# A two-layer decoder trunk on one core: where a schedule puts the third branch's norm steps, the compression steps and the tiles of stages 8 to 11

## The chip, the cores and the metric

The kernel runs on one core of one Trainium2 chip. The metric is device time in microseconds (us) for one execution of the whole program, taken from the first to the last work of that core. The engines are named PE (TensorE, matrix products), PEld (its weight loads), DVE (VectorE), ACT (ScalarE), POOL (GpSimd) and SP (SyncE, which only issues DMA transfers here).

## The reference, cut to what matters

Two layers. In each, h is the RMS-normed input (512 tokens x 1024), and one wide projection of h feeds three token mixers: A (8 heads with a forget gate), B (compressed, selected and windowed attention, 8 query heads on 2 key groups) and C (4 heads, each the difference of two softmax maps). Each mixer's output is multiplied by a SiLU gate, projected to 1024 columns, weighted by a sigmoid gate and summed; then an output projection, a residual and a gated per-layer embedding.

```
k_cmp = compress_blocks(kcb..., w1_k, w2_k)      # silu(flat @ w1 + b1) @ w2, likewise for v
w = prob[:, :, 0] - lam * prob[:, :, 1]          # branch C, lam = exp(..) - exp(..) + lam_init
yc = rmsnorm(out, subln_g) * (1.0 - lam_init)    # the third branch's norm, per head
merged = g0 * (ya @ w_br_a) + g1 * (yb @ w_br_b) + g2 * (yc @ w_br_c)
```

All products are to have fp32 accuracy. The kernel splits each operand into a high and a low part of a faster type and multiplies three times: high by high, low by high, high by low.

## The kernel before

**Tiles.** The dense work is cut into tiles of 128 output columns over all 512 tokens. A tile of a projection of h has 8 steps, a tile of a branch projection (`bra`, `brb`, `brc`) 4; a step is three matmuls of 512 columns (lines 729 to 731). A tile of the compression's hidden layer (`w1k`, `w1v`) has 4 steps of two matmuls of 256 columns (lines 742 and 743). Weights come from DRAM into `raw` (4 slots); ACT copies them to `w_hi` (line 1031, function `hi`), DVE subtracts to get `w_lo` (line 1260, function `lo`), each in two halves, into 2 slots. The weights of tile t+2 are therefore split only when tile t has ended. The output banks `D0` and `D1` alternate too: tile t+2 can't begin before tile t has been taken out of its bank (`arena`, `zs`, `rx` and `th` are such destinations; a `brb` tile is taken out by two DVE instructions, lines 1435 and 1439, which multiply by the gate and add to `acc`).

**Stages.** Twelve stages, 0 to 3 for branch A, 4 to 7 for B, 8 to 11 for C. In a stage the attention rows of one head pair run (`S` scores, softmax row maximum on DVE line 1511 and exponential on ACT line 1146, `T` transposes of the probabilities and their copy `pT`, line 541, `V` the product with the values, `N` the scaling into `y_q`), and between them the steps of the dense tiles that `dense_tiles` lists for the stage. Branch C also has `CB` (four DVE instructions, lines 1522 to 1525, that combine the two maps), `SQ` (ACT squares), `MS` (DVE takes the mean square, line 1575, and POOL raises it to the power -1/2, line 687), `YN` (four small DVE instructions and one multiplication of `y_q`, lines 1579 to 1583), `Y` (PE transposes `y_q`, line 934, DVE writes `y_f`) and `YS` (ACT and DVE split `y_f` into `y_hi` and `y_lo`, lines 1165 and 1597). Tiles whose columns are rotated (`qb`, `ksb`, `kwb`, `qc`, `kc`) have `swap` (4 DMAs and a POOL product) and `rot` later on.

**What sets the order.** `make_schedule` writes one list of items for all engines, and each engine issues its part of the list strictly in that order. A stage is cut into ticks, one per row (stage 11 has 7 more). Each tick places its row items and, spread between them, a share of the stage's dense steps by weight: a `w1k` or `w1v` step weighs 1, any other 2. Items in `late`, `newton` and `vq` are due at a tick; items in `follow` are due after a number of dense steps. So how much PE work lies between two items, and what stands before a given item in the queues of DVE and ACT, both come from this function.

Of the kernel before, what the change touches and what calls it, by code (L numbers as in the profile page):

```python
# [1723 lines left out]
```

## Time and profile before

| | us |
|---|---|
| median of 3 runs | 1573.89 (1573.87 to 1575.48) |
| the profiled execution, its own time | 1574.78 |
| its span, first to last instruction | 1573.0 |
| PE busy | 1514.2 (96%) |
| DVE busy | 941.8 (60%) |
| ACT busy | 638.6 (41%) |
| POOL busy | 73.4 (5%) |

PE is busy nearly all the time, so its idle time and the stretches at a lower granted clock are all that an order of work can change. A row of a timeline gives the start, the duration, the engine, the line and the operands, and in brackets how long the engine had been idle and what ended that. Matmul rows last longer than the distance between them, since matmuls overlap. Layer 1 runs from about 15 to 790 us, layer 2 after it, with the same order of items.

### The profile page before, as it was taken

Reading aid. Unit: us, or ns where it says so; the run is one execution under the profiler, and the core shown is the slowest. Engines: PE = TensorE matmul, PEld = TensorE weight load, DVE = VectorE, ACT = ScalarE, POOL = GpSimd, SP = SyncE. Lnnn points to the kernel's source line nnn. Section 1 sums busy time; section 2 is a strip of 40 time slices with the busy share of each in tenths; the row PEclk is TensorE's granted clock in tenths of the full one; section 3 lists DMA queues with packets and bytes.
Section 4 is the critical chain, followed back from the end, with each engine's and each line's share of the span. In section 5 each row is a group of like instructions: output and inputs, shape, how many; then the busy total and the mean of one; then the engine's idle time right before and its main releaser. Section 6 shows DMA issues by size and latency. Waiting matters only on the chain.

```text
span 1573.0 us, 22642 instructions
## 1 busy us (share of the span) xinstructions
PE 1514.2 (96%) x7957; PEld 1212.5 (77%) x7957; DVE 941.8 (60%) x2205; ACT 638.6 (41%) x1492; POOL 73.4 (5%) x79
## 2 busy tenths in 40 slices
PE   8999999999999999999999999999999999999997
PEld 6777777777777777878787777787887777788785
DVE  6856655555557666455576657655555666754544
ACT  6533433333344443343444334333434434433343
POOL 1000000000000000000200000000000000000011
PEclk9999999999999999999999999999999999999998
DMA  7223322222223332332442324222222233233222
GB/s 194 81 81 88 94 71 58 60 68 61 66 63 94 88 81 74 93 114 59 113 108 68 101 67 109 71 52 66 61 61 74 68 94 84 71 89 105 87 78 77
DMA packets 250300, 129.47 MB, mean 82 GB/s; under 512 B 45691, under 2 KB 245973, under 8 KB 250197
## 3 DMA queue, kind: packets, MB, share of 16 engines
q1 hardware_dynamic: 250196, 128.13, 30.5%
q8 instruction: 60, 0.98, 0.3%
q14 instruction: 44, 0.35, 0.1%
HBM read 118.67 MB, written 2.10 MB: 77 GB/s over the span
## 4 chain that ended last, share of the span: by engine, by line
PE 78%; DVE 8%; issue 6%; ACT 4%; DMA 1%; POOL 1%; SPq 1%; ACTq 0%; POOLq 0%; DVEq 0%
PE D L729 22%; PE D L731 19%; PE D L730 19%; PE Ob L917 7%; PE S L876 4%; PE T L895 3%; DVE w_lo L1260 2%; ACT w_hi L1031 1%; ACT probs L1146 1%; PE Ob L922 1%; DMA rs<-rx 1%; PE Mb L934 1%; SPq L630 1%; DVE h_lo L1602 1%; PE Mb L843 1%
## 5 line engine op out<-in xcount | busy, mean ns | idle before, releaser
L729 PE MATMUL D<-h_hi,w_hi 128*128 128x512 f32 x1264 | 544.6, 431 | 17.3 <-DVE zs L1408 4.9
L731 PE MATMUL D<-h_lo,w_hi 128*128 128x512 f32 x1264 | 496.8, 393 | 0.0
L730 PE MATMUL D<-h_hi,w_lo 128*128 128x512 f32 x1264 | 495.6, 392 | 0.0
L1260 DVE TENSOR_TENSOR w_lo<-raw,w_hi 128x512 fp32r<-128x512 f32 (+2 forms) x504 | 297.3, 631 | 315.5 <-ACT w_hi L1031 315.3
L1031 ACT ACTIVATE w_hi<-raw 128x512 fp32r<-128x512 f32 (+2 forms) x504 | 266.3, 575 | 315.4 <-PE D L731 314.4
L729 PEld LDWEIGHTS D<-h_hi,w_hi 128*128 128x128 f32 x1264 | 238.8, 189 | 82.0 <-issue 20.6
L1146 ACT ACTIVATE probs<-probs,nmax 128x128 f32<-128x128 f32 (+3 forms) x256 | 141.9, 555 | 376.3 <-DVE nmax L1511 376.2
L731 PEld LDWEIGHTS D<-h_lo,w_hi 128*128 128x128 f32 x1264 | 238.0, 188 | 53.4
L730 PEld LDWEIGHTS D<-h_hi,w_lo 128*128 128x128 f32 x1264 | 239.7, 190 | 30.8 <-issue 0.5
L1511 DVE CUSTOM_DVE_ANT_0 probs<-S,maskb 128x128 f32<-128x128 f32 (+3 forms) x256 | 115.2, 487 | 57.3 <-PE S L876 35.8
L541 DVE COPY pT<-T 128x128 f32<-128x128 f32 (+3 forms) x160 | 77.5, 486 | 50.0 <-PE T L895 49.6
L917 PEld LDWEIGHTS Ob<-v_b,pT 128*128 128x128 f32 x640 | 90.8, 191 | 11.9 <-ACT pT L539 0.9
L895 PE MATMUL T<-ident,probs 128*128 128x128 f32 x560 | 97.7, 272 | 1.7 <-ACT probs L1146 1.7
L876 PE MATMUL S<-arena 64*128 64x384 f32 (+3 forms) x768 | 93.8, 349 | 0.9 <-DVE arena L1404 0.9
L729 PE MATMUL D<-y_hi,w_hi 128*128 128x512 f32 x224 | 94.0, 420 | 0.4 <-DVE y_lo L1597 0.4
L895 PEld LDWEIGHTS T<-ident,probs 128*128 128x128 f32 x560 | 72.6, 140 | 27.1 <-ACT probs L1146 4.0
L876 PEld LDWEIGHTS S<-arena 64*128 64x128 f32 x768 | 57.1, 185 | 45.6 <-issue 41.2
L731 PE MATMUL D<-y_lo,w_hi 128*128 128x512 f32 x224 | 87.9, 392 | 0.0
L730 PE MATMUL D<-y_hi,w_lo 128*128 128x512 f32 x224 | 87.5, 390 | 0.0
L917 PE MATMUL Ob<-v_b,pT 128*128 128x64 f32 x640 | 85.4, 264 | 0.0
L684 POOL TENSOR_TENSOR rb<-rs,sinT 128x512 f32<-128x512 f32 x28 | 36.1, 1290 | 1012.9 <-DMA rs<-rx 595.2
L917 PEld LDWEIGHTS Ob<-v_ac,pT 128*128 128x128 f32 x480 | 66.9, 192 | 16.3 <-DVE pT L541 9.1
(241 smaller groups left out, 1497.8 us busy)
## 6 DMA issues: line engine op xcount, KB each, us to landing
raw<-in_w_in_dram SPq DMA_DIRECT2D x124, 512.0 KB, 3.9
raw<-in_w_in_dram SPq DMA_DIRECT2D x32, 256.0 KB, 3.7
raw<-in_w_out_dram SPq DMA_DIRECT2D x16, 512.0 KB, 4.0
raw<-in_w_ple_gate_dram SPq DMA_DIRECT2D x16, 512.0 KB, 4.2
rs<-rx SPq DMA_DIRECT2D x80, 64.0 KB, 2.0
raw<-in_cmp_w_k_dram SPq DMA_DIRECT2D x8, 512.0 KB, 3.7
raw<-in_cmp_w_v_dram SPq DMA_DIRECT2D x8, 512.0 KB, 3.8
raw<-in_w_br_a_dram SPq DMA_DIRECT2D x16, 256.0 KB, 2.8
```

What stands on the lines that cost most here:

```text
L541: eng.tensor_copy(pT[:, k % 2, 0:n], Tr[k % 2][:, 0:n]).then_inc(M["pt_dve_s"], 1)
L684: pool.tensor_tensor(rb[:], rs[:], sinT[:], ALU.mult).then_inc(M["pool_rot"], 1)
L729: pe.matmul(o, w_hi[:, sl, cs], hi[:, k, :], start=(k == 0), stop=False)
L730: pe.matmul(o, w_lo[:, sl, cs], hi[:, k, :], start=False, stop=False)
L731: ins = pe.matmul(o, w_hi[:, sl, cs], lo[:, k, :], start=False, stop=last)
L876: ins = pe.matmul(Sc[h][:, 0:n], qx[ps, qs], kx[ps, 0:n], start=(step == 0), stop=last)
L895: ins = pe.transpose(Tr[k % 2][:, j * P:(j + 1) * P], src[:, j * P:(j + 1) * P], ident[:])
L917: ins = pe.matmul(Ob[:, oc], pT[:, k % 2, j * P:(j + 1) * P], vs(j), start=(j == 0), stop=(j == i))
L1031: A(w_hi[:, sl, half], raw[:, ring(L, t, RAW), half], ACT.Copy).then_inc(M["act_hi"], 1)
L1146: A(probs[:, r % NP_, 0:n], probs[:, r % NP_, 0:n], ACT.Exp, scale=-1.0, bias=nmax[:, r % 8:r % 8 + 1], accum_out=sums[:, u % 2, i, c:c + ...
L1260: TT(w_lo[:, sl, half], raw[:, ring(L, t, RAW), half], f(w_hi[:, sl, half]), ALU.subtract).then_inc(M["dve_lo"], 1)
L1511: dve.tensor_tensor_reduce(probs[:, r % NP_, 0:n], Sc[r % 2][:, 0:n], maskb[:, S - n:S], -1.0, 3.0e38, ALU.add, ALU.min, nmax[:, r % 8:r % ...
```

## The change

The code is the same in what it computes. Five things differ.

1. Stages 7 to 11 hold other tiles. `kc 1` moves from stage 8 to stage 7. Stages 8, 9 and 10 go from 48 dense steps to 36 each, and stage 11 from 32 to 60. The last tile is now `brb 7`, and `zc 3` stands in the middle of stage 11, so that `Y` and `YS` of unit 11 come inside the list and the extra wait on line 945 goes.
2. `MS` and `YN` of branch C are placed 3 and 5 dense steps after the last `N` of a unit (before: both one tick later), `Y` still two ticks later; for unit 11 too.
3. The last lambda arithmetic on DVE becomes an item `lam` of its own, 30 steps after the `fg` tile instead of 7. ACT's exponential for it stays at `gates`.
4. A `w1k` or `w1v` step weighs 4, not 1, in the share of a tick. `ht` and `kcmp` come 12 and 16 steps after `w1k 3`, not 4 and 7.
5. A `brb` tile waits for the addition of the one before it.

```
-    st[7] = [("qc", 0), ("zb", 3), ("kc", 0), ("mga", 6), ("bra", 6), ("mga", 7), ("bra", 7)]
-    st[8] = [("qc", 1), ("mgb", 0), ("kc", 1), ("zc", 0), ("brb", 0), ("mgb", 1), ("brb", 1)]
-    st[9] = [("qc", 2), ("mgb", 2), ("kc", 2), ("zc", 1), ("brb", 2), ("mgb", 3), ("brb", 3)]
...
-    st[11] = [("mgb", 6), ("brb", 6), ("mgb", 7), ("brb", 7), ("zc", 3)]
+    st[7] = [("qc", 0), ("zb", 3), ("kc", 0), ("mga", 6), ("bra", 6), ("kc", 1), ("mga", 7), ("bra", 7)]
+    st[8] = [("qc", 1), ("mgb", 0), ("zc", 0), ("brb", 0), ("mgb", 1)]
+    st[9] = [("qc", 2), ("brb", 1), ("kc", 2), ("zc", 1), ("mgb", 2)]
...
+    st[11] = [("brb", 3), ("mgb", 4), ("brb", 4), ("zc", 3), ("mgb", 5), ("brb", 5), ("mgb", 6), ("brb", 6),
+              ("mgb", 7), ("brb", 7)]
...
-                follow.extend([[3, ("lf1", t)], [7, ("gates", t)], [9, ("lf2", t)]])
+                follow.extend([[3, ("lf1", t)], [7, ("gates", t)], [9, ("lf2", t)], [30, ("lam", t)]])
...
-                follow.extend([[4, ("ht", t)], [7, ("kcmp", t)]])
+                follow.extend([[12, ("ht", t)], [16, ("kcmp", t)]])
...
-            weight.append(weight[-1] + (1 if tiles[t][0] in ("w1k", "w1v") else 2))
+            weight.append(weight[-1] + (4 if tiles[t][0] in ("w1k", "w1v") else 2))
...
-                            late.append((tick + 1, ("MS", u)))
-                            newton.append((tick + 1, ("YN", u)))
-                            if u < UNITS - 1:
-                                late.append((tick + 2, ("Y", u)))
+                            late.append((tick + 2, ("Y", u)))
...
                     follow.append([1, ("SQ", part[1])])
+                    if i == NQ - 1:
+                        follow.extend([[3, ("MS", u)], [5, ("YN", u)]])
...
-    items += [("Y", UNITS - 1), ("YS", UNITS - 1)]
...
-                                if j == 0:
-                                    pe.wait_ge(M["dve_evac"], dve_evac.after(T0 - 2))
...
+                                if not first and n:
+                                    dve.wait_ge(M["dve_acc"], n)
```

DVE's queue in stage 9, around the norm of unit 8. `msq` is the norm's small arithmetic, `y_q` the unit's output, `coef` and `probs` the combination of the next unit's two maps, `rc` and `arena` a rotated tile. Before:

```order
L1523 TENSOR_TENSOR coef<-coef,lams 128x1
L1524 TENSOR_SCALAR probs<-probs,coef 128x256
L1525 SCALAR_TENSOR_TENSOR probs<-probs,coef 128x256
L1500 TENSOR_TENSOR rc<-rc,rb 128x512
L1502 TENSOR_TENSOR arena<-rc,arena 128x512
L541 COPY pT<-T0 128x128
L1575 TENSOR_SCALAR msq<-msq 128x4
L1579 TENSOR_TENSOR msq<-msq 128x4
L1580 TENSOR_TENSOR msq<-msq 128x4
L1581 TENSOR_SCALAR msq<-msq 128x4
L1582 TENSOR_TENSOR msq<-msq 128x4
L1583 TENSOR_TENSOR y_q<-y_q,msq 128x512
```

The same place after the change, from the end of tile `brb 1` (its `w_lo`, `qf` and `acc`):

```order
L1258 TENSOR_TENSOR w_lo<-raw,w_hi 128x512 x2
L1435 SCALAR_TENSOR_TENSOR qf<-th,D0 128x512
L1439 TENSOR_TENSOR acc<-acc,qf 128x512
L1523 RECIPROCAL coef<-sums 128x2
L1524 TENSOR_TENSOR coef<-coef,lams 128x1
L1525 TENSOR_SCALAR probs<-probs,coef 128x256
L1526 SCALAR_TENSOR_TENSOR probs<-probs,coef 128x256
L1576 TENSOR_SCALAR msq<-msq 128x4
L541 COPY pT<-T0 128x128
L1580 TENSOR_TENSOR msq<-msq 128x4
L1581 TENSOR_TENSOR msq<-msq 128x4
L1582 TENSOR_SCALAR msq<-msq 128x4
```

The rotated tile's two instructions have gone behind the norm, and the four that end a `brb` tile now stand before it.

DVE's queue at the norm of unit 11, near the end of stage 11. Before:

```order
L1575 TENSOR_SCALAR msq<-msq 128x4
L1260 TENSOR_TENSOR w_lo<-raw,w_hi 128x512 x2
L1435 SCALAR_TENSOR_TENSOR qf<-th,D1 128x512
L1439 TENSOR_TENSOR acc<-acc,qf 128x512
L1579 TENSOR_TENSOR msq<-msq 128x4
L1580 TENSOR_TENSOR msq<-msq 128x4
L1581 TENSOR_SCALAR msq<-msq 128x4
L1582 TENSOR_TENSOR msq<-msq 128x4
L1583 TENSOR_TENSOR y_q<-y_q,msq 128x512
L1597 TENSOR_TENSOR y_lo<-y_f,y_hi 128x512 x3
```

After:

```order
L1258 TENSOR_TENSOR w_lo<-raw,w_hi 128x512 x2
L1576 TENSOR_SCALAR msq<-msq 128x4
L1580 TENSOR_TENSOR msq<-msq 128x4
L1581 TENSOR_TENSOR msq<-msq 128x4
L1582 TENSOR_SCALAR msq<-msq 128x4
L1583 TENSOR_TENSOR msq<-msq 128x4
L1584 TENSOR_TENSOR y_q<-y_q,msq 128x512
L1258 TENSOR_TENSOR w_lo<-raw,w_hi 128x256 x2
L1435 SCALAR_TENSOR_TENSOR qf<-th,D0 128x512
L1439 TENSOR_TENSOR acc<-acc,qf 128x512
L1593 SCALAR_TENSOR_TENSOR y_f<-Mb,gsc,zs 128x512
```

Nothing is left between the mean square and the four small instructions, and `Y` follows inside the list; before it came behind all dense steps of the stage.

PE's queue around the first hidden tile `w1k 0`, in layer 1. Before, the row `Ob` is `V` and the two rows `S` are the next unit's scores:

```order
L917 MATMUL Ob<-v_ac,pT 128x64 x3
L742 MATMUL D<-w_hi,arena 128x256
L743 MATMUL D<-w_lo,arena 128x256
L742 MATMUL D<-w_hi,arena 128x256
L743 MATMUL D<-w_lo,arena 128x256
L742 MATMUL D<-w_hi,arena 128x256
L743 MATMUL D<-w_lo,arena 128x256
L742 MATMUL D<-w_hi,arena 128x256
L743 MATMUL D<-w_lo,arena 128x256
L876 MATMUL S<-arena 128x128 x6
L882 MATMUL S<-ck,selr 128x128 x2
L729 MATMUL D<-h_hi,w_hi 128x512
```

After, from the end of tile `za 0` on:

```order
L731 MATMUL D<-h_lo,w_hi 128x512
L876 MATMUL S<-arena 128x512 x6
L882 MATMUL S<-ck,selr 128x512 x2
L895 MATMUL T<-ident,probs 128x128 x3
L742 MATMUL D<-w_hi,arena 128x256
L743 MATMUL D<-w_lo,arena 128x256
L917 MATMUL Ob<-v_ac,pT 128x64 x3
L742 MATMUL D<-w_hi,arena 128x256
L743 MATMUL D<-w_lo,arena 128x256
L895 MATMUL T<-ident,probs 128x128 x4
L917 MATMUL Ob<-v_ac,pT 128x64 x3
L742 MATMUL D<-w_hi,arena 128x256
```

The scores of the unit's last row, two transposes and a `V` have come in behind `za 0`; the four-matrix transpose needs the probabilities of the scores four items ahead of it.

## Rows read from the trace of the kernel before

**Rows 1.** The page: busy time by engine, and one group (busy, mean ns | idle before).

```profile
PE 1514.2 (96%) x7957; PEld 1212.5 (77%) x7957; DVE 941.8 (60%) x2205; ACT 638.6 (41%) x1492; POOL 73.4 (5%) x79
...
L729 PE MATMUL D<-y_hi,w_hi 128*128 128x512 f32 x224 | 94.0, 420 | 0.4 <-DVE y_lo L1597 0.4
```

**Rows 2.** Waits of PE, whole span: us in total, times, longest us.

```profile
PE Mb L934 <- DVE y_q L1583: 7.4, 6, 1.3
...
PE D L729 <- DVE zs L1408: 4.9, 4, 2.5
PE Ob L917 <- DVE pT L541: 4.8, 5, 1.8
PE Mb L816 <- DVE tmp L1430: 4.6, 2, 2.3
PE D L729 <- DVE arena L1404: 3.7, 5, 1.3
```

**Rows 3.** Timeline of PE, stage 11 and the step behind it, layer 1.

```profile
603.77 0.38 PE L917 MATMUL Ob<-v_ac,pT 128*128 128x128 f32 x1 [1.81 <-DVE pT L541]
...
617.79 0.49 PE L729 MATMUL D<-h_hi,w_hi 128*128 128x512 f32 x1 [1.00 <-ACT th L1093]
```

**Rows 4.** Timeline of all engines where a `brb` tile ends, stage 9.

```profile
497.24 0.39 PE L730 MATMUL D<-y_hi,w_lo 128*128 128x512 f32 x1
...
497.47 0.39 PE L731 MATMUL D<-y_lo,w_hi 128*128 128x512 f32 x1
...
497.95 1.15 ACT L1031 ACTIVATE w_hi<-raw 128x512 fp32r<-128x512 f32 x2 [1.43 <-PE D L731]
...
498.62 1.29 DVE L1260 TENSOR_TENSOR w_lo<-raw,w_hi 128x512 fp32r<-128x512 f32 x2 [1.25 <-ACT w_hi L1031]
...
499.83 0.68 DVE L1435 SCALAR_TENSOR_TENSOR qf<-th,D 128x512 f32<-128x512 f32 x1
...
500.54 0.69 DVE L1439 TENSOR_TENSOR acc<-acc,qf 128x512 f32<-128x512 f32 x1
```

**Rows 5.** Timeline of all engines at the norm of unit 8, stage 9.

```profile
514.52 0.16 DVE L1522 RECIPROCAL coef<-sums 128x2 f32<-128x2 f32 x1
...
515.29 0.49 DVE L1525 SCALAR_TENSOR_TENSOR probs<-probs,coef 128x256 f32<-128x256 f32 x1
...
517.85 0.79 PE L876 MATMUL S<-arena 64*128 64x384 f32 x6
...
517.94 0.16 DVE L1575 TENSOR_SCALAR msq<-msq 128x4 f32<-128x4 f32 x1
...
519.23 0.16 DVE L1579 TENSOR_TENSOR msq<-msq 128x4 f32<-128x4 f32 x1 [1.13 <-POOL msq L687]
...
520.86 0.63 PE L934 MATMUL Mb<-ident,y_q 128*128 128x128 f32 x4 [1.33 <-DVE y_q L1583]
```

**Rows 6.** Timelines of DVE and ACT at the end of `za 0`.

```profile
84.26 0.69 DVE L1511 CUSTOM_DVE_ANT_0 probs<-S,maskb 128x512 f32<-128x512 f32 x1 [0.38 <-PE S L882]
...
85.00 0.72 ACT L1146 ACTIVATE probs<-probs,nmax 128x512 f32<-128x512 f32 x1 [2.91 <-DVE nmax L1511]
...
89.45 1.15 ACT L1031 ACTIVATE w_hi<-raw 128x512 fp32r<-128x512 f32 x2 [2.93 <-PE D L731]
...
91.32 0.68 DVE L1408 SCALAR_TENSOR_TENSOR zs<-th,D 128x512 f32<-128x512 f32 x1
```

**Rows 7.** Timelines of DVE, PE and ACT: the compression's input, and `w1k 3`.

```profile
73.40 3.00 DVE L1355 TENSOR_TENSOR v_b<-D,par 64x248 f32<-64x248 f32 x8
...
139.66 0.47 PE L729 MATMUL D<-h_hi,w_hi 128*128 128x512 f32 x1 [0.27 <-DVE arena L1404]
...
139.89 0.51 ACT L1146 ACTIVATE probs<-probs,nmax 128x256 f32<-128x256 f32 x1 [1.29 <-DVE nmax L1511]
```

**Rows 8.** Stretches: length, busy PE, PEld, DVE, ACT, POOL, then granted clock, DMA, GB/s.

```profile
197.00:204.00 7.00, 5.99 (x21) 5.01 (x22) 3.82 (x9) 0.89 (x2) 0.00 (x0) 0.76 0.66 150
918.00:924.00 6.00, 5.67 (x24) 4.52 (x25) 2.26 (x8) 0.00 (x0) 0.00 (x0) 0.72 0.28 81
```

**Rows 9.** Timeline of all engines, stage 8.

```profile
482.49 1.29 POOL L684 TENSOR_TENSOR rb<-rs,sinT 128x512 f32<-128x512 f32 x1 [11.20 <-DMA rs<-rx]
...
483.08 1.25 DVE L1597 TENSOR_TENSOR y_lo<-y_f,y_hi 128x512 fp32r<-128x512 f32 x1 [1.65 <-ACT y_hi L1165]
```

More of the change, by code:

```diff
@@ L76, in dense_tiles @@
     st[6] = [("qb", 3), ("vc", 2), ("zb", 2), ("vc", 3), ("mga", 4), ("bra", 4), ("mga", 5), ("bra", 5)]
-    st[7] = [("qc", 0), ("zb", 3), ("kc", 0), ("mga", 6), ("bra", 6), ("mga", 7), ("bra", 7)]
-    st[8] = [("qc", 1), ("mgb", 0), ("kc", 1), ("zc", 0), ("brb", 0), ("mgb", 1), ("brb", 1)]
-    st[9] = [("qc", 2), ("mgb", 2), ("kc", 2), ("zc", 1), ("brb", 2), ("mgb", 3), ("brb", 3)]
-    st[10] = [("qc", 3), ("mgb", 4), ("kc", 3), ("zc", 2), ("brb", 4), ("mgb", 5), ("brb", 5)]
-    st[11] = [("mgb", 6), ("brb", 6), ("mgb", 7), ("brb", 7), ("zc", 3)]
+    st[7] = [("qc", 0), ("zb", 3), ("kc", 0), ("mga", 6), ("bra", 6), ("kc", 1), ("mga", 7), ("bra", 7)]
+    st[8] = [("qc", 1), ("mgb", 0), ("zc", 0), ("brb", 0), ("mgb", 1)]
+    st[9] = [("qc", 2), ("brb", 1), ("kc", 2), ("zc", 1), ("mgb", 2)]
+    st[10] = [("qc", 3), ("brb", 2), ("kc", 3), ("zc", 2), ("mgb", 3)]
+    st[11] = [("brb", 3), ("mgb", 4), ("brb", 4), ("zc", 3), ("mgb", 5), ("brb", 5), ("mgb", 6), ("brb", 6),
+              ("mgb", 7), ("brb", 7)]
     return st
@@ L174, in emit_group @@
             if kind == "fg":
-                follow.extend([[3, ("lf1", t)], [7, ("gates", t)], [9, ("lf2", t)]])
+                follow.extend([[3, ("lf1", t)], [7, ("gates", t)], [9, ("lf2", t)], [30, ("lam", t)]])
             if kind == "brb" and tiles[t][1] == 7:
-                for u in range(8, 11):
+                for u in range(8, UNITS):
                     follow.append([1 + u - 8, ("YS", u)])
@@ L188, in make_schedule @@
         emit_group(g)
-    vq, late, newton = [], [], []
+    vq, late = [], []
     tick = 0
@@ L226, in make_schedule @@
                         if branch(u) == "C":
-                            late.append((tick + 1, ("MS", u)))
-                            newton.append((tick + 1, ("YN", u)))
-                            if u < UNITS - 1:
-                                late.append((tick + 2, ("Y", u)))
+                            late.append((tick + 2, ("Y", u)))
                         else:
                             late.append((tick + 1, ("Y", u)))
-            while newton and newton[0][0] <= tick:
-                parts.append(newton.pop(0)[1])
             if s == 8 and 1 <= j <= 4:
@@ L242, in make_schedule @@
                 if part[0] == "N" and branch(part[1] // NQ) == "C":
+                    u, i = divmod(part[1], NQ)
                     follow.append([1, ("SQ", part[1])])
+                    if i == NQ - 1:
+                        follow.extend([[3, ("MS", u)], [5, ("YN", u)]])
                     follow.sort(key=lambda f: f[0])
@@ L259, in make_schedule @@
         items.append(follow.pop(0)[1])
-    items += [("Y", UNITS - 1), ("YS", UNITS - 1)]
-    assert not late and not newton and not vq and ti == len(prob_rows)
+    assert not late and not vq and ti == len(prob_rows)
     where = {x: n for n, x in enumerate(items)}
     for u in range(8, UNITS):
-        assert where[("SQ", NQ * u + NQ - 1)] < where[("MS", u)], u
+        assert where[("SQ", NQ * u + NQ - 1)] < where[("MS", u)] < where[("YN", u)] < where[("Y", u)], u
+        assert where[("Y", u)] < where[("YS", u)], u
+    assert tiles[-2][0] == "mgb" and tiles[-1][0] == "brb"
     for u in range(1, UNITS):
@@ L1461, in _ @@
                             link(TT(gsc[:], par[:, PAR_SUB + L:PAR_SUB + L + 1], lconst[:, 1:2], ALU.mult))
+                        elif what == "lam":
                             dve.wait_ge(M["act_lam"], L + 1)
```

## The prediction, made before the changed kernel was run

> **What bounds the kernel now.** I read the page first, then the list of waits of PE, then the timelines round each wait. The page shows PE busy 96% of the span, the other engines 60% or less [rows 1]; no work of PE is added or taken away by the change, so only its waits and its clock can move. The list of waits shows what they are [rows 2]: six before the transpose of `y_q` (7.4 us), four for `zs`, five for `pT`, two for the hidden layer's `tmp` (4.6), five for `arena`. In stage 11 and right behind it stand one of 1.81 for a copy of probabilities and one of 1.00 for a gate tile [rows 3], and both layers have them. The stretches view shows two dips of the granted clock, to means of 0.76 and 0.72 [rows 8]. That is TensorE at its lower level (1.2 GHz) for part of the stretch, behind a wait of 2.5 for `zs` in layer 1 and of 2.3 for `tmp` in layer 2 [rows 2]. Each costs (1 - 0.76) x 7 = (1 - 0.72) x 6 = 1.7 us.
>
> The question for every moved item is whether the engine that feeds PE there is free. Where a tile ends, ACT and DVE are not, and that is the core of my sum. A matmul of 512 columns starts 0.23 after the one before (497.24, 497.47), so a step of three takes 0.70, and PE is free of the `brb` tile at 497.70; ACT's split starts at 497.95, DVE's two `w_lo` at 498.62, `qf` at 499.83, and `acc` ends at 501.23 [rows 4]. So **DVE is free of a `brb` tile 3.5 us after PE is**.
>
> **The norm of units 8 and 9 (stages 9 and 10).** From the end of `brb 1`, DVE has: the tile's end 3.5; `coef` to `probs` 1.26 (514.52 to 515.78); the mean square 0.16; its wait for POOL, which lasts from 518.10 to 519.23 and hides the 0.28 copy of `pT`, 1.13; from there to PE's transpose 1.63 (519.23 to 520.86) [rows 5]. Sum 7.7. PE has from the same point to `Y`: seven steps, 4.9, one `S` pass of 0.8 and a small transpose of 0.1 [rows 4, 5]: 5.9. The wait becomes 1.8; before it is 1.33 [rows 5]. Before, the rotation's two instructions stood in front of the mean square; now a `brb` tile's end does, and PE has a shorter tick to cover it. Lower bound 0, if DVE starts the tile's end without delay and the copies overlap more than the rows show; upper 2.6, with POOL's product on top (below).
>
> The same shorter ticks leave DVE busy through the rest of the stage. Stages 9 and 10 lose 12 of 48 steps, 8.4 us of PE time each, but only an `mgb` and a `brb` tile's ends on DVE (1.3 and 2.2). Followed on, DVE copies the probabilities of the third row 0.9 us after PE wants them, behind `zs`, a rotation and a `coef` group. The rows give no such wait in these stages before, so its bounds are 0 and 2; I take 0.9. Together (1.8 + 0.9 - 1.33) = +1.37 per stage, x4: **+5.5**.
>
> **Stage 8.** `brb 0` waits for `y_lo` of unit 7: 0.2 per layer before [rows 1]. `YS 7` comes one step later and there are fewer steps between; the queue in front of it (a `y_lo`, two maxima, the rotation with its turn through ACT, `N`, the square, `y_hi`) sums to 7.9 after the end of `mgb 0`, PE arrives at 6.9. Wait 1.0, bounds 0.2 and 1.8: **+1.6** for both layers.
>
> **Stage 11.** Removed per layer: the 1.81, a 0.4 of the same kind, the 1.0 before `Y 10` and the 1.00 at the first `mgc` [rows 2, 3]; 4.3 in all. With four steps per tick instead of two the copies come in time. `zc 3` no longer ends the stage, and the new last wait, for `y_lo` of unit 11 before the first `brc`, is hidden: the tile's end and four `y_lo` take 5.3, the 8 steps of `mgc` 5.6. That cover is thin; if DVE is 0.5 late it costs 0.2. Added: `Y 10` has four steps fewer work before it than DVE needs (lo 2.2, `coef` 1.26, norm 2.9 against 4.4 of PE): 1.9. `Y 11` stands right behind `brb 6`: DVE has the two `w_lo` of `mgb 7`, free 2.2 after PE [rows 4], then 0.16 + 1.13 + 1.63 [rows 5], 5.1 in all, and PE only four steps, 2.8. Wait 2.3; before, it lay behind the whole of `zc 3` and cost nothing. Sum 4.2 against 4.3: **-0.3** for both layers, bounds -6 and +1.
>
> **Compression.** *Before `qa 2`, beside `w1k 0`*: a wait of 0.6 for `zs` goes (one of the four [rows 2]). But the transpose of the unit's last row now stands between two hidden steps. Its probabilities need `zs` (ends 92.00, 2.8 after PE left `za 0`), then a maximum of 0.69, then an exponential of 0.72 [rows 6]: 4.3. PE has `S` 1.3, transposes 0.3, `V` 0.65, two hidden steps 0.6: 2.8. Wait 1.4, so +0.8 per layer, +1.7. *`w1k 1`*: 0.4 of work comes in front of a wait for `arena`: -0.8 for both. *`w1k 3`*: `ht` 12 steps on removes 2.3 per layer [rows 2]. In its place the transposes of the row just scored stand in the hidden tile; they need an exponential that ends at 140.40, while before the next tile started at 139.66 [rows 7]; PE ends 1.1 later than before. Net -2.4. *`w1v`*: 0.43 of `V` in front of each wait for `zs`, and 0.2 near `ht`: -1.3. *`kcb`*: scores now stand right behind the tile whose eight DVE instructions take 3.00 [rows 7]; two waits of 0.6 replace one of 0.6 (layer 1) or two of 0.55 (layer 2): +0.7. Sum **-2.1**, bounds -9 (every wait named here gone) and +3.
>
> **Clock.** Without the 2.3 wait the dip of layer 2 should go; the wait for `zs` in layer 1 shrinks from 2.5 only to 2.0, and I leave that dip: **-1.7**, bounds -3.4 and +3.4 (the 2.3 before `Y 11` causes one per layer).
>
> **Lambda, and the wait on the addition.** 0. DVE's next instruction behind the lambdas waited for ACT's split in any case, which stands behind ACT's exponential, and that has not moved. The addition is always done.
>
> **A rule against it.** POOL's `rb` product ran from 482.49 to 483.78, and `y_lo`, which other rows show at 0.69, took 1.25 beside it and ended 0.55 after it [rows 9]. The Trainium skill, GPSIMD Engine Reference, section "Specifications", says that POOL's interfaces to SBUF are shared with VectorE and that they contend where a DVE instruction has two SBUF inputs. By that, with `rb` of `qc 2` now falling on the `acc` addition (two SBUF inputs), the norm waits of stages 9 and 10 would be up to 0.6 longer, +2.4 in all; without it, nothing. The sum stands without.
>
> **The sum**, against the profiled execution's own 1574.78: +5.5 +1.6 -0.3 -2.1 -1.7 = +3.0, so 1577.8; the median of the runs shown lies 0.9 lower, so 1576.9.
>
> **Rivals.** *A, DVE is not the late engine.* If the ends of `brb` tiles slip in front as fast as the steps, the norm waits go (-7.4), stage 11's copies and gate waits too (-6.4), with compression and clock as above (-3.8): 1556. For it: that DVE is busy only 60%, and DVE stands idle for over 1 us in front of most splits. Against it: those idle times lie before a tile's end, and the items in question all stand behind one. A half of it, where the norm waits halve (-3.7) and stages 8 to 10 get no other new ones, stage 11, compression and clock as in the sum (-4.1), gives 1566. *B, a pile-up, slower.* The place is the tick in stages 9 and 10 in which `zs`, a rotation and `coef` meet. It decides once DVE's queue of a stage with its waits is longer than PE's 33 us; I count 29. Each us of excess then stays, four times, with `rb` on top and a clock dip behind `Y 11` in each layer: 1573.9 +3.0 +2.4 +3.4 = 1582.7, more where the excess is larger. *C, no effect*: the waits only change place, each as long as it was: 1574.
>
> **How the numbers follow.** What a measurement can tell from no change is 0.2%, 3.1 us. My forecast, a sum of 0 to +6, gets 0.45, half of it within 0.2% and half beyond. Rival A with its half gets 0.28, B 0.15, C 0.12. Slower: 0.225 + 0.15, and a little of C, 0.39; same: 0.225 + 0.10, 0.33; faster 0.28. The range runs from 1563, between A and its half, to 1583, where B ends; the forecast's own is 1573 to 1580.
>
> **What would show it.** In the profile after: waits of PE for `y_q` of 1.8 in stages 9 and 10, 1.9 and 2.3 in stage 11, 8 of them; waits for `pT` of about 0.9 once in each of stages 9 and 10 and none of 1.8 in stage 11; the wait of the first `mgc` gone; one of 1.4 for `probs` beside `w1k 0` and about as much beside `w1k 3`; none for `tmp` of 2.3; one dip of the clock. I am wrong if waits for `y_q` sum to less than 7.4, or if those in stage 11 fall by over 2 per layer.

## The result, and the profile after

| | us |
|---|---|
| before, median of 7 runs beside the changed kernel | 1575.48 (1573.87 to 1578.6) |
| changed kernel, median of 7 runs | 1585.53 (1582.76 to 1592.05) |
| ratio, 95% interval | 1.0072 (1.0059 to 1.0086) |
| profiled executions, before and after | 1574.78 and 1591.31 |
| their mean granted clock | 0.995 and 0.986 |

The change costs 0.7%, outside the range I gave. The seven runs of the changed kernel lie further apart than those of before, and their time goes with the clock: 1591.3 and 1592.1 us at a mean of 0.986, 1588.4 at 0.988, 1585.0 to 1585.5 at 0.991, 1582.8 at 0.992. The profiled execution, 1591.31 us, is the second longest of the seven, 5.8 us above the median, so its profile shows more of the lower clock than a run at the median has.

The page shows the same work, 11.5 us more of it busy on PE. It answers to [rows 1]:

```profile
PE 1525.7 (96%) x7957; PEld 1220.2 (77%) x7957; DVE 946.6 (60%) x2205; ACT 638.4 (40%) x1492; POOL 74.4 (5%) x79
```

The instructions are equal in number, so the added busy time is not work; the granted clocks further down say what it is. The waits of PE, which answer to [rows 2] (us in total, times, longest us):

```profile
PE Mb L934 <- DVE y_q L1584: 18.2, 8, 2.6
PE T L895 <- ACT probs L1144: 6.9, 6, 1.4
...
PE D L729 <- DVE arena L1402: 2.3, 3, 1.3
PE Ob L917 <- DVE pT L541: 2.1, 4, 0.6
...
PE D L729 <- DVE y_lo L1598: 1.9, 2, 0.9
PE D L729 <- DVE zs L1406: 1.8, 2, 0.9
...
PE Ob L917 <- DVE y_q L1559: 1.2, 2, 0.6
```

The `tmp` line (4.6) and the wait of the first `mgc` [rows 3] are gone, `zs`, `pT` and `arena` have shrunk; `y_q` has gone from 7.4 to 18.2 and `probs` from 1.7 to 6.9. All idle times of PE over 0.06 us, summed, are 48.8 us before and 53.9 after: +5.1.

The other 11.4 of the 16.5 us are in the stretches view. Columns as in [rows 8], the last but two being the granted clock; the first two rows are the same times as those of [rows 8], now at full clock, as is everything from 99 to 515 us and from 877 to 1293; the others stand behind waits:

```profile
197.00:204.00 7.00, 6.12 (x36) 4.81 (x34) 4.50 (x10) 1.83 (x4) 0.00 (x0) 1.00 0.66 150
918.00:924.00 6.00, 4.61 (x35) 3.90 (x35) 3.72 (x11) 2.63 (x7) 0.00 (x0) 1.00 0.05 10
...
88.00:100.00 12.00, 10.58 (x55) 8.93 (x55) 7.05 (x19) 3.67 (x11) 0.00 (x0) 0.72 0.32 87
514.00:520.00 6.00, 5.52 (x21) 4.59 (x22) 5.19 (x13) 3.35 (x8) 0.00 (x0) 0.72 0.13 32
551.00:557.00 6.00, 5.25 (x19) 4.36 (x20) 5.18 (x11) 3.35 (x8) 0.00 (x0) 0.72 0.11 28
868.00:880.00 12.00, 10.58 (x52) 9.00 (x51) 6.35 (x18) 3.55 (x10) 0.00 (x0) 0.72 0.29 88
...
1364.00:1370.00 6.00, 5.19 (x19) 4.43 (x20) 5.82 (x15) 1.71 (x6) 0.00 (x0) 0.72 0.34 87
1394.00:1400.00 6.00, 4.70 (x16) 3.89 (x17) 3.67 (x9) 0.00 (x0) 0.00 (x0) 0.72 0.44 125
```

A mean of 0.72 over 6 us is 3.4 us at 1.2 GHz, worth 1.7 us of work at 2.4 GHz; the two rows of 12 us hold twice that. With 1292 to 1298 and 1329 to 1335, which read alike, there are ten such units, against two before. Eight more at up to 1.7 are up to 13.7; the busy time shows 11.5. Four of the ten stand behind norm waits of 2.60 to 2.65, four (two in a row, twice) behind the waits of 1.42 beside `w1k 0`, and one each, in layer 2 alone, behind the 1.63 before `Y 10` and the 2.19 before `Y 11`.

What they stand behind, with the norm of unit 8 first (all engines, stage 9; it answers to [rows 5]), then the transpose beside `w1k 0`:

```profile
510.51 0.16 DVE L1576 TENSOR_SCALAR msq<-msq 128x4 f32<-128x4 f32 x1
...
510.75 1.01 POOL L687 TENSOR_TENSOR msq<-msq,halfs 128x4 f32<-128x4 f32 x1 [35.04 <-DVE msq L1576]
...
511.73 1.26 POOL L684 TENSOR_TENSOR rb<-rs,sinT 128x512 f32<-128x512 f32 x1
511.80 1.21 DVE L1580 TENSOR_TENSOR msq<-msq 128x4 f32<-128x4 f32 x1 [0.93 <-POOL msq L687]
...
513.64 0.69 DVE L1584 TENSOR_TENSOR y_q<-y_q,msq 128x512 f32<-128x512 f32 x1
...
514.48 0.63 PE L934 MATMUL Mb<-ident,y_q 128*128 128x128 f32 x4 [2.65 <-DVE y_q L1584]
...
90.55 0.66 PE L895 MATMUL T<-ident,probs 128*128 128x128 f32 x4 [1.42 <-ACT probs L1144]
```

The first small product on `msq`, 0.16 before, lasts 1.21 here: it runs beside POOL's `rb`. That is 1.05 more in a wait of 2.65.

### The profile page after: what moved, and what is told of

The parts are those of the page before. It is cut to its first block, busy times and chain, and to the rows that moved or that the text cites. A ratio compares the mean times of both kernels' runs of the same rounds, so it can differ in the third digit from the quotient of the medians.

```text
span 1589.5 us, 22608 instructions
## 1 busy us (share of the span) xinstructions
PE 1525.7 (96%) x7957; PEld 1220.2 (77%) x7957; DVE 946.6 (60%) x2205; ACT 638.4 (40%) x1492; POOL 74.4 (5%) x79
## 4 chain that ended last, share of the span: by engine, by line
PE 75%; issue 10%; DVE 9%; ACT 4%; POOL 1%; DMA 1%; SPq 1%; ACTq 0%; POOLq 0%; DVEq 0%
PE D L729 21%; PE D L731 18%; PE D L730 18%; PE Ob L917 6%; PE S L876 4%; PE T L895 3%; DVE w_lo L1258 3%; ACT w_hi L1029 2%; PE Ob L922 1%; PE Mb L934 1%; DVE v_b L1353 1%; ACT probs L1144 1%; DVE h_lo L1603 1%; PE Mb L843 1%; POOL msq L687 1%
## 5 line engine op out<-in xcount | busy, mean ns | idle before, releaser
L729 PEld LDWEIGHTS D<-h_hi,w_hi 128*128 128x128 f32 x1264 | 241.1, 191 | 73.1 <-issue 16.2
L917 PEld LDWEIGHTS Ob<-v_b,pT 128*128 128x128 f32 x640 | 90.8, 191 | 11.9 <-ACT pT L539 1.0
L917 PEld LDWEIGHTS Ob<-v_ac,pT 128*128 128x128 f32 x480 | 68.3, 195 | 13.8 <-DVE pT L541 5.8
```

Of the source, the lines that this page charges most:

```text
L729: pe.matmul(o, w_hi[:, sl, cs], hi[:, k, :], start=(k == 0), stop=False)
L917: ins = pe.matmul(Ob[:, oc], pT[:, k % 2, j * P:(j + 1) * P], vs(j), start=(j == 0), stop=(j == i))
```

## The experiments

Twelve kernels, each run 4 to 12 times beside the kernel before on the same chip. Three chips took part; the kernel before had medians of 1574.5 to 1574.7 us on all three.

| kernel | median | ratio (95%) | profile: clock, idle of PE |
|---|---|---|---|
| `comp_only` | 1573.62 | 0.9983 (0.9970 to 0.9995) | 0.996, 46.6 |
| `ht_only` | 1566.75 | 0.9944 (0.9931 to 0.9957) | 0.993, 43.3 |
| `stages_only` | 1594.36 | 1.0123 (1.0108 to 1.0137) | 0.988, 56.4 |
| `swap_early` | 1590.11 | 1.0093 (1.0079 to 1.0108) | 0.986, 54.0 |
| `rb_late` | 1577.49 | 1.0017 (1.0003 to 1.0030) | 0.996, 49.8 |
| `norm_pad` | 1590.76 | 1.0100 (1.0087 to 1.0113) | 0.989, 57.1 |
| `brb_last` | 1572.18 | 0.9980 (0.9969 to 0.9991) | 0.991, 47.1 |
| `stage11_even` | 1563.44 | 0.9916 (0.9903 to 0.9929) | 0.996, 40.3 |
| `norm_early` | 1559.13 | 0.9898 (0.9885 to 0.9911) | 0.997, 36.7 |
| `norm_early_brb5` | 1572.93 | 0.9983 (0.9975 to 0.9992) | 0.994, 45.5 |
| `norm_pad_half` | 1582.35 | 1.0040 (1.0027 to 1.0053) | 0.990, 51.2 |
| `rb_late_w1` | 1572.75 | 0.9983 (0.9974 to 0.9993) | 0.997, 46.3 |

Each profile shows one execution. That of `comp_only` is the second shortest of its twelve, those of `rb_late` and `rb_late_w1` are the shortest of theirs, so these three show less of the lower clock than their medians contain.

### Which part costs: `comp_only`, `ht_only`, `stages_only`

`comp_only` is the kernel before with this; `ht_only` has the first pair of lines alone:

```
-                follow.extend([[4, ("ht", t)], [7, ("kcmp", t)]])
+                follow.extend([[12, ("ht", t)], [16, ("kcmp", t)]])
...
-            weight.append(weight[-1] + (1 if tiles[t][0] in ("w1k", "w1v") else 2))
+            weight.append(weight[-1] + (4 if tiles[t][0] in ("w1k", "w1v") else 2))
```

`stages_only` is the changed kernel with both pairs undone, and `MS` and `YN` one tick behind the last `N` as before.

> The kernel before with the compression part alone (hidden steps weigh 4, ht and kcmp 12 and 16 steps behind w1k 3). Theory 1 (the loss is mostly the granted clock, behind single waits of PE): PE's idle time falls by about 2.8 us over both layers, as it fell in these stretches of the profile after, but dips stand behind w1k 0's 1.4 wait in both layers, four units of 3.41 us in place of two, +3.4: a profile of 1575 to 1576, ratio 0.999 to 1.002. Theory 2 (the waits alone decide, dips fall by chance): -2.8, ratio 0.998. Theory 3 (this part carries most of the loss): ratio over 1.004.

> The kernel before with ht and kcmp alone moved to 12 and 16 steps behind w1k 3, hidden steps weigh 1 as before. Theory 1: the wait of 2.3 us for tmp goes in both layers (-4.6, perhaps 0.5 of it back in V's wait), the dip of layer 2 behind it goes too (-1.7): ratio 0.996 to 0.998, clock one unit of 3.41 us at the lower level at most. Theory 2 (waits alone): -4.1 to -4.6, 0.997, and the dip of layer 2 stays or turns up elsewhere. If the transposes now in the hidden tile wait for the exponential, 1 to 1.4 per layer comes back: 0.999.

> The changed kernel with the compression part undone and the norms of the third branch placed by ticks as before: what is left is the table of stages 7 to 11 (and the lambdas' place, worth 0). Theory 1: PE's idle time in these stages grows by 7.3 us over both layers as it did in the profile after, and up to six units of 3.41 us at the lower clock (1.7 each) stand behind the norm waits: +9 to +17 in the profile, ratio 1.006 to 1.010. Theory 2 (waits alone): +7.3, ratio 1.0046, clock as before. Theory 3 (compression carries the loss): ratio under 1.003.

The stages carry the loss, more of it than the whole change: +19.7 us. The compression part gains 0.2%, and its half, `ht` and `kcmp` alone, gains 0.6%, more than any of my theories had. In its profile PE idles 5.5 us less, as the waits of 2.3 for `tmp` are gone in both layers and the long one for `zs` is 1.4; the stretch at the lower clock behind `tmp` is gone, but two stand in stage 11, behind waits of 1.8 for `pT`. The weight of 4 gives 0.4% back. The two parts multiply to 1.0106, the whole change is 1.0072: `stages_only` also undoes the placing of the norm by steps, so by this difference that placing gives back some 0.3% (norm waits of 2.60 to 2.65 in the changed kernel, 2.81 to 2.85 in `stages_only`). It was not run alone, nor were `lam` and the wait for the addition. The waits of PE in `stages_only`, then in `comp_only`:

```profile
PE Mb L936 <- DVE y_q L1586: 19.3, 8, 2.8
PE Ob L704 <- DMA y_q<-in_final_g_dram: 5.4, 1, 5.4
PE Mb L818 <- DVE tmp L1430: 4.6, 2, 2.3
```

```profile
PE Mb L934 <- DVE y_q L1583: 7.3, 6, 1.3
PE T L895 <- ACT probs L1146: 6.8, 6, 1.4
```

`stages_only` idles 7.6 us more than before and holds nine units at 1.2 GHz in place of two, 7 x 1.7 = 11.9; the sum is 19.5, and its profile is 19.6 longer. So waits and clock together, theory 1, account for it, and the waits alone, theory 2 (1.0046), do not; still, 1.0123 lies above theory 1's range, since seven units came where it allowed six. `comp_only` does not decide. No unit stood behind `w1k 0`'s wait in its profile, 1.42 as in the changed kernel, and theory 2's 0.998 is the ratio. But the profile belongs to the four of its twelve runs that took 1567.6 to 1568.8 us at a clock of 0.995 to 0.997; the other eight took 1573.4 to 1574.0 at 0.992 or 0.993. Those 5.7 us are what three or four units at the lower clock would cost (an estimate, from 1.7 each), so most runs may well have had the units of theory 1. None of them was profiled.

### POOL's product: `swap_early` and `rb_late`

```
-                follow.append([8, ("swap", t)])
+                follow.append([5 if kind == "qc" and tiles[t][1] > 1 else 8, ("swap", t)])
```

> The changed kernel with POOL's rb product of qc 2 and qc 3 put 3 steps earlier in POOL's order, ahead of the power of units 8 and 9, so that it cannot run beside the norm's arithmetic on DVE. Collision theory: the first product on msq falls from 1.21 to about 0.16 us, the norm waits of stages 9 and 10 from 2.65 to 1.6 to 1.8, four of them, -3.4 to -4; if dips of the clock need such long waits, up to six units of 1.7 us go with them: ratio to the kernel before 1.000 to 1.004, against 1.007 for the changed kernel. Rival (the 1.21 has another cause, or rb only collides elsewhere, with w_lo or the mask's maxima): waits stay at 2.4 to 2.65 and the ratio at 1.006 to 1.008.

The ratio is the rival's and a little beyond it, yet the product on `msq` fell to 0.16 as the collision theory wants. What it lost, another instruction gained (all engines, stage 9):

```profile
506.75 2.39 DVE L1258 TENSOR_TENSOR w_lo<-raw,w_hi 128x512 fp32r<-128x512 f32 x2 [1.64 <-ACT w_hi L1029]
...
507.29 1.30 POOL L684 TENSOR_TENSOR rb<-rs,sinT 128x512 f32<-128x512 f32 x1 [31.59 <-DMA rs<-rx]
...
512.84 0.16 DVE L1580 TENSOR_TENSOR msq<-msq 128x4 f32<-128x4 f32 x1 [0.93 <-POOL msq L687]
```

The pair of `w_lo`, 1.29 in [rows 4], takes 2.39: 1.1 more, which arrives at the norm undiminished (waits of 2.65 to 2.70). Which of the two is held up goes by who starts first. In stage 8 of the changed kernel (all engines) `y_lo`, also with two operands in SBUF, began 0.13 before `rb`:

```profile
473.87 0.69 DVE L1598 TENSOR_TENSOR y_lo<-y_f,y_hi 128x512 fp32r<-128x512 f32 x1 [0.74 <-ACT y_hi L1163]
...
474.00 1.71 POOL L684 TENSOR_TENSOR rb<-rs,sinT 128x512 f32<-128x512 f32 x1 [21.66 <-DMA rs<-rx]
...
474.67 1.05 DVE L1524 TENSOR_TENSOR coef<-coef,lams 128x1 f32<-128x1 f32 x1
```

`y_lo` kept its 0.69 and `rb` took 1.71 instead of 1.29; the next DVE product of two SBUF operands, 0.16 in other places, lasted until `rb` had ended. `rb_late` instead lets POOL wait in front of `rb`:

```
                             pool.wait_ge(M["sw_ld"], 64 * n)
+                            if tiles[it[1]][0] == "qc" and tiles[it[1]][1] > 1:
+                                pool.wait_ge(M["yqc_s"], tiles[it[1]][1] - 1)
```

> The changed kernel, but POOL waits with rb of qc 2 and qc 3 until the norm's last product on DVE is done. With rb 3 steps earlier it hit DVE's second w_lo half instead (0.69 became 1.78) and the norm wait stayed 2.65. Collision theory: rb now lies beside maxima that read PSUM, the first product on msq lasts 0.16 and w_lo 0.69; the norm waits of stages 9 and 10 fall to 1.6 to 1.8 (four of them, -4); the units of 3.41 us at the lower clock behind them go too if they need waits over 2 us, -7: ratio to the kernel before 1.000 to 1.006. If waits of 1.6 draw the clock down as well (as the 1.63 before Y 10 did in layer 2), only -4: 1.006 to 1.008. Rival (rb costs DVE 1.1 wherever it stands): waits stay at 2.6, ratio 1.007 to 1.009.

The timeline of all engines at the norm of unit 8 in `rb_late`:

```profile
509.84 0.16 DVE L1582 TENSOR_TENSOR msq<-msq 128x4 f32<-128x4 f32 x1 [0.94 <-POOL msq L689]
...
511.24 0.55 DVE L1514 CUSTOM_DVE_ANT_0 probs<-S,maskb 128x384 f32<-128x384 f32 x1
...
511.46 1.28 POOL L686 TENSOR_TENSOR rb<-rs,sinT 128x512 f32<-128x512 f32 x1 [1.65 <-issue]
511.47 0.63 PE L936 MATMUL Mb<-ident,y_q 128*128 128x128 f32 x4 [1.60 <-DVE y_q L1586]
```

Beside `rb` DVE now takes maxima of scores in PSUM, at their usual 0.55, and nothing is stretched. The norm waits of stages 9 and 10 are 1.55 to 1.60 instead of 2.60 to 2.65. The stretches behind them are at full clock:

```profile
510.00:516.00 6.00, 4.53 (x24) 3.87 (x25) 4.67 (x13) 3.46 (x8) 1.28 (x1) 1.00 0.02 5
545.00:551.00 6.00, 4.73 (x25) 4.03 (x26) 4.70 (x12) 3.46 (x8) 1.28 (x1) 1.00 0.06 15
```

One wait on POOL takes four times 1.05 us of waiting away, 4.2 us, and the median falls by 8.0 from that of the changed kernel (1585.53 to 1577.49; the ratio from 1.0072 to 1.0017). The rest, about 4, goes with the clock. This profile, at 1572.87 us and 0.996, is the shortest of twelve: six of the others took 1579.0 to 1581.7 us at 0.990 to 0.993. So waits of 1.6 do not rule the lower clock out; it comes less often.

### Is it the wait that brings the clock down: `norm_pad`, `norm_pad_half`

The kernel before, its table and all; only the first small product of the norm is repeated, 7 times or 3 times more:

```
-                            link(TT(msq[:, 3, :], msq[:, 2, :], msq[:, 2, :], ALU.mult))
+                            for _ in range(8):
+                                link(TT(msq[:, 3, :], msq[:, 2, :], msq[:, 2, :], ALU.mult))
```

> The kernel before, with the first small product of each norm done 8 times in place of once (same result, 7 x 0.20 = 1.4 us more on DVE). Table and all else as before; only the waits before Y 8, 9 and 10 grow from 1.33, 1.33 and 1.03 to about 2.6, 2.6 and 2.4, six waits, +8. Clock theory (a single long wait of PE is what the lower clock follows, in these stages also without the new table): up to six units of 3.41 us at the lower level appear behind them, +5 to +10 on top: ratio 1.008 to 1.012, granted clock 0.987 to 0.990. Rival (the dips came from the denser DVE and PE mix of the new table, or by chance): +8 only, ratio 1.005, clock 0.993 to 0.995.

> The kernel before with the first small product of each norm done 4 times (3 x 0.20 more on DVE): the waits before Y 8, 9 and 10 grow from 1.33, 1.33 and 1.03 to about 1.9, 1.9 and 1.7, six waits, +3.6. Clock theory by the lengths seen so far (stretches at the lower clock stood behind every wait of 2.4 to 2.85, behind half of those of 2.1 to 2.3, behind few of 1.4 to 1.8): two to four units of 3.41 us more, or none in some executions, so +3.6 to +10, ratio 1.002 to 1.006, with runs apart by whole units. Rival (time follows the wait alone): 1.0023, runs as close as those of before. Rival (any wait over 1.5 draws the lower clock): 1.008.

The waits of `norm_pad`, then the stretches behind four of its six long ones (all six have one):

```profile
PE Mb L934 <- DVE y_q L1584: 17.4, 8, 2.7
```

```profile
521.00:527.00 6.00, 5.76 (x22) 4.76 (x23) 5.65 (x14) 1.71 (x6) 1.28 (x1) 0.72 0.36 92
565.00:571.00 6.00, 5.06 (x18) 4.25 (x19) 5.82 (x15) 1.71 (x6) 1.28 (x1) 0.72 0.20 56
599.00:605.00 6.00, 5.97 (x26) 4.65 (x26) 4.70 (x13) 2.13 (x8) 0.00 (x0) 0.72 0.15 44
1299.00:1305.00 6.00, 5.64 (x21) 4.69 (x22) 5.74 (x14) 1.71 (x6) 1.30 (x1) 0.72 0.36 93
```

The first of these stretches, by the same place of the program, is at full clock in the kernel before:

```profile
521.00:527.00 6.00, 6.00 (x30) 5.01 (x30) 4.16 (x13) 2.07 (x7) 1.29 (x1) 1.00 0.43 112
```

Waits of 2.42 to 2.70 in place of 1.03 to 1.33 cost 8.3 us as waits and 16.2 us in the median. Half the lengthening (waits of 1.62 to 1.92) cost 7.7 us, of which 2.4 are idle time of PE, and in its profile three of the six had a unit at the lower clock behind them (two more stand behind other waits). So the price of a wait is itself and, with a frequency that rises with its length, another 1.7 us. That needs neither the new table of stages nor anything else of the change.

### Other tables: `brb_last`, `stage11_even`, `norm_early`, `norm_early_brb5`

`brb_last` is the changed kernel with the following, stage 7 as before, and `mgb 3` at the head of stage 11:

```
+    st[8] = [("qc", 1), ("mgb", 0), ("kc", 1), ("zc", 0), ("brb", 0)]
+    st[9] = [("qc", 2), ("mgb", 1), ("kc", 2), ("zc", 1), ("brb", 1)]
+    st[10] = [("qc", 3), ("mgb", 2), ("kc", 3), ("zc", 2), ("brb", 2)]
```

> The changed kernel with another table of the same evenness: stage 7 as before; stage 8 qc 1, mgb 0, kc 1, zc 0, brb 0; stage 9 qc 2, mgb 1, kc 2, zc 1, brb 1; stage 10 likewise with 3, 2, 3, 2, 2; mgb 3 heads stage 11. Stages 8 to 10 have 36 steps as in the changed kernel, but an mgb tile, whose end is ACT's, stands ahead of the norm in place of a brb tile, whose end holds DVE for 3.5 us. My theory (it is the brb end ahead of the norm that makes the wait): norm waits of stages 9 and 10 of 0 to 1.0 in place of 2.65, no dip behind them, 4 x 1.7 to 2.6 less and up to 6 less of clock: ratio 0.997 to 1.003. Rival (fewer steps between the norm and Y are what makes the wait): waits of 1.8 to 2.6 and ratio 1.004 to 1.008.

The norm waits of stages 9 and 10 are gone, with still 36 steps per stage: the end of the `brb` tile ahead of the norm was the cause, not the number of steps. (The product on `msq` still lasts 1.01 beside `rb` there, and PE does not wait for it.) But six waits of 2.1 for a rotation have come, one in each of stages 8 to 10 of both layers, and the four units at the lower clock in this profile stand behind three of them:

```profile
PE S L876 <- DVE arena L1503: 12.6, 6, 2.1
```

In the timeline of all engines the rotation of `kc 1` stands behind a `zs` and a copy of `pT`:

```profile
484.84 0.68 DVE L1406 SCALAR_TENSOR_TENSOR zs<-th,D 128x512 f32<-128x512 f32 x1
...
485.44 0.55 DVE L541 COPY pT<-T 128x384 f32<-128x384 f32 x1
...
485.91 0.68 DVE L1501 TENSOR_TENSOR rc<-rc,rb 128x512 f32<-128x512 f32 x1
486.62 0.63 ACT L1137 ACTIVATE arena<-rc 128x512 fp32r<-128x512 f32 x1 [2.02 <-DVE rc L1501]
...
487.28 0.69 DVE L1503 TENSOR_TENSOR arena<-rc,arena 128x512 fp32r<-128x512 f32 x1 [0.70 <-ACT arena L1137]
...
488.03 0.55 PE L876 MATMUL S<-arena 64*128 64x128 f32 x6 [2.10 <-DVE arena L1503]
```

`stage11_even` leaves stages 7 to 10, the norms and the weight as before, keeps points 3 and 5 of the change, moves `ht` and `kcmp`, and has the ends of the last `brb` tiles behind the rows' work:

```
-    st[11] = [("mgb", 6), ("brb", 6), ("mgb", 7), ("brb", 7), ("zc", 3)]
+    st[11] = [("mgb", 6), ("zc", 3), ("brb", 6), ("mgb", 7), ("brb", 7)]
```

> A candidate: ht and kcmp at 12 and 16 steps, hidden steps weigh 1, stages 7 to 10 and the norms by ticks as before, and stage 11 as mgb 6, zc 3, brb 6, mgb 7, brb 7, so that the ends of brb tiles on DVE come behind the rows' work; Y 11 last. Theory: ht_only's 7 to 8 us, and of stage 11's waits (0.41, 1.81, 1.00 per layer) most goes, -5 to -6.4, and the dips that ht_only showed in stage 11 of both layers go too (-3); Y 10's 1.03 stays: ratio 0.988 to 0.991. Rival (the first brc waits for y_lo of unit 11, whose chain now has only the 5.6 us of mgc as cover; or the brb 7 end delays the first mgc): 1 to 2 us per layer back, ratio 0.992 to 0.994.

The ratio falls between theory and rival. The wait of 1.81 is down to 0.1, that of the first `mgc` is gone; an earlier copy of `pT` waits 1.15 (0.41 before) and the first `brc` 0.82. In sum PE waits 1.1 us less per layer there than before, where I had hoped for 2.5 to 3.2, and no stretch at the lower clock is left in the profile between 45 and 1530 us.

`norm_early` adds, for units 8 and 9, `MS` 2 steps and `YN` 5 steps behind the last `N`, so that the rotation stands between them:

```
+                    if part[1] % NQ == NQ - 1 and part[1] // NQ < 10:
+                        follow.extend([[2, ("MS", part[1] // NQ)], [5, ("YN", part[1] // NQ)]])
```

> The candidate stage11_even, with the norms of units 8 and 9 by steps, mean square 2 steps behind the last row's normalization (ahead of the rotation of qc) and the rest 5 steps behind it (behind the rotation). Theory: the rotation's 2.1 us on DVE now hide POOL's power (1.13 of DVE's wait before), so the waits for y_q in stages 9 and 10 fall from 1.33 to about 0.2, four of them, -4.5, and no dip is left to lose: ratio to the kernel before 0.988 to 0.990, against 0.9916. Rival (another item, the copy of pT or the max of the next row, is late there instead, since T and S stand in other places): -2 or less, 0.990 to 0.992.

The timeline of DVE and POOL at the norm of unit 8, stage 9:

```profile
509.12 0.17 DVE L1582 TENSOR_SCALAR msq<-msq 128x4 f32<-128x4 f32 x1 [0.47 <-ACT cs_ L1162]
...
509.37 1.01 POOL L693 TENSOR_TENSOR msq<-msq,halfs 128x4 f32<-128x4 f32 x1 [4.64 <-DVE msq L1582]
...
510.00 0.48 DVE L1532 SCALAR_TENSOR_TENSOR probs<-probs,coef 128x256 f32<-128x256 f32 x1
510.40 0.68 DVE L1507 TENSOR_TENSOR rc<-rc,rb 128x512 f32<-128x512 f32 x1
511.83 0.69 DVE L1509 TENSOR_TENSOR arena<-rc,arena 128x512 fp32r<-128x512 f32 x1 [0.75 <-ACT arena L1143]
512.44 0.16 DVE L1586 TENSOR_TENSOR msq<-msq 128x4 f32<-128x4 f32 x1
```

POOL's power ends at 510.38, under the combination of the two maps on DVE (`coef` and `probs`), and the small products follow the rotation without an idle time ([rows 5] have one of 1.13). The norm waits are 0.50 instead of 1.33 (0.2 forecast); 1559.13 us is the best of all kernels here, 1.0% under the kernel before.

`norm_early_brb5` moves `brb 5` behind `mgb 6`, into stage 11.

> As norm_early, with brb 5 moved from the end of stage 10 to behind mgb 6 in stage 11. Theory: stage 11 gets 36 steps in 15 ticks and DVE reaches the copy of pT (1.15 late in both layers of stage11_even) in time, -1 to -2; but brb 5's end holds DVE for 3.5 us ahead of Y 10, whose wait grows from 1.05 to 2 or more, and the lower clock may follow that: +2 to +5. I expect the second to win: ratio 0.989 to 0.992, not better than norm_early. If not, 0.987.

Worse than either number: the end of `brb 5` ahead of the norm of unit 10 makes a wait of 3.5, with a unit at the lower clock, in both layers. The copy that waited 1.15 is in time, as forecast, but a later one waits 1.60 and 1.92 in its place, the second with a unit behind it. It is the changed kernel's mistake in one tile, 13.8 us for it.

### The two halves together: `rb_late_w1`

`rb_late` with the hidden steps at weight 1.

> rb_late (the changed kernel, POOL's rb behind the norm) with hidden steps weighing 1 again, ht and kcmp still at 12 and 16 steps. comp_only and ht_only differ by this weight alone, 0.9983 against 0.9944. If that carries over: the waits of 1.42 and 1.38 for probabilities beside w1k 0 and w1k 3 go in both layers, about 2.5 of idle time net, and the stretches at the lower clock that stood behind them in the changed kernel: ratio 0.997 to 0.999, against 1.0017. Rival (the weight matters only with the old stages 8 to 11): 1.001 to 1.003.

The weight costs 0.3 to 0.4% with either set of stages; at weight 1 the waits of 1.42 and 1.38 for `probs` are gone.

### Waits and the lower clock over all profiles

In the profiles of these twelve kernels and of before and after, between 45 and 1530 us, every one of the 47 stretches at 1.2 GHz begins between 0.5 us before and 1.6 us after the end of a wait of PE of over 1.4 us:

| length of the wait | waits | with a stretch |
|---|---|---|
| 2.4 to 3.5 | 21 | 21 |
| 2.0 to 2.4 | 25 | 11 |
| 1.5 to 2.0 | 38 | 11 |
| 1.0 to 1.5 | 137 | 4 |

The last four are the wait of 1.42 beside `w1k 0`, in both layers of the changed kernel and of `swap_early`; the same wait stood without one in `comp_only`, `rb_late` and `brb_last`. Both layers have it in each kernel, so that is 4 of 10, and each of the four is of double length. What else decides there is open; it was not tried. The counts come from one execution per kernel, and many of the waits are the same place in kernels that differ little, so they are frequencies for this program and no more.

## Why the prediction failed

**Which engine, which waits: right.** DVE is free of a `brb` tile 3.5 us after PE, and the norm behind it is late: `brb_last` takes the tile away and the wait with it. The end waits of stages 8 and 11 came at 0.94 (forecast 1.0), 1.63 for `Y 10` (1.9) and 2.19 for `Y 11` (2.3); beside `w1k 0` 1.42 (1.4), beside `w1k 3` 1.38; the `tmp` wait and the first `mgc`'s went. The sum of my waits was +4.7 us, the idle time of PE grew by 5.1.

**The clock term: wrong, and it is most of the miss.** I had "-1.7, bounds -3.4 and +3.4", one dip fewer, and allowed one behind `Y 11` in each layer. In the profiled execution eight units more came; at the median the change costs 10 us, of which 5.1 are idle time, so about 5 are left for the clock where the sum had -1.7. The step that failed was to read the two dips of [rows 8] as tied to two waits, of 2.5 and 2.3, and not to ask the same of the new waits that the sum itself put in: 1.8 in each of stages 9 and 10, and 1.4 beside `w1k 0`. Of the ten units four stand behind norm waits of 2.60 to 2.65, a length behind which a unit came in all 21 cases of the table; that is 6.8 us. `norm_pad` shows the mechanism with nothing else changed. Another four stand behind the two waits of 1.42, forecast at 1.4; why they came there, when the other 133 waits of 1.0 to 1.5 had none, stays open. The waits of 1.4 to 2.2 have a unit in some executions and not in others, which fits the changed kernel's runs lying 9 us apart, at clocks of 0.986 to 0.992.

The dip that I left in was wrong too: the wait for `zs` in layer 1, 2.0 forecast, measured 0.89, and nothing stood behind it. In `norm_pad` and `norm_pad_half`, with the order of before at that place, it is 2.32 and 1.29, so its 2.5 was partly that one execution's.

**The norm waits of stages 9 and 10: 1.8 forecast, 2.65 measured.** The excess is POOL's `rb`: with it out of the way the waits are 1.55 to 1.60 (`rb_late`), a little under my 1.8. I had worked out a norm wait longer by "up to 0.6", for another place: the `acc` addition. It fell on the first product on `msq`, a 128x4 instruction, which lasted as long as `rb`: 1.05 more. By the rule that I weighed (the Trainium skill, GPSIMD Engine Reference, "Specifications": POOL shares its SBUF interfaces with VectorE, and they contend where a DVE instruction has two SBUF inputs) the trace agrees in three places: that product, `y_lo` in [rows 9] and `w_lo` in `swap_early` have two SBUF inputs each and are stretched, the maxima over PSUM in `rb_late` are not. All three started after `rb`; the `y_lo` of the changed kernel's stage 8, which started first, was not stretched. The product `rb` belonged into the sum with 4 x 1.05, and it is what took the waits from 1.6, behind which `rb_late`'s profile shows no lower clock, to 2.65, behind which there always was one.

**The third row's copy: 0.9 forecast, four times; measured 0.6 twice and 0.1 twice.** That error, -2.2, takes back most of the norm's +3.4. Two slips in the sum's arithmetic are smaller: 4.9, 0.8 and 0.1 make 5.8 and not 5.9, and 4.2 against 4.3, twice, is -0.2 and not -0.3; together 0.5 us.

**Compression: -2.1 forecast; idle of PE there -1.7 and -1.1, but `comp_only` less `ht_only` shows that the weight costs 0.4%.** I had booked the step's weight and the later `ht` as one sum; apart, they have opposite signs.

**Rivals.** B had the right members, `rb` on top and dips, with too few dips and in the wrong proportion; its end of 1582.7 lies under the median. A (1556) was wrong for this table, since the norm waits grew; `norm_early`, whose norm waits did shrink, reaches 1559.

## What to carry to other kernels

Here, with the matrix engine busy 96% of the time, a single wait had two prices: its own length and, from about 1.5 us on more and more often, 1.7 us of a lower clock behind it; two waits of 1.3 were far cheaper than one of 2.6. Runs of one kernel then differ by several units, so a single profile can show none of them or all. Place a norm, a softmax or any chain that the matrix engine will want behind tiles that another engine closes, and give a helper engine's part (here POOL's power) a neighbour on DVE to hide under. A POOL product over SBUF (1.3 us) cost a DVE instruction with two SBUF operands that started behind it 0.6 to 1.1 us, most of the time that the two overlapped, so hang it on a place where DVE reads PSUM.
